# Two norms and the first block of the projection behind each: chunk by chunk through four open groups

## What is computed

```python
for i in range(DEPTH):
    mod_x = (silu_c @ w_mod[i] + b_mod[i])[:, None, :]
    mod_c = silu_cc @ w_mod[i] + b_mod[i]
    sh_x, sc_x, g_x = jnp.split(mod_x, 3, axis=-1)
    sh_c, sc_c, g_c = jnp.split(mod_c, 3, axis=-1)
    hx = rms_norm(x, norm_g[i]) * (1.0 + sc_x) + sh_x
    hc = rms_norm(ctx, norm_g[i]) * (1.0 + sc_c) + sh_c
```

## Time and profile before

| what | value |
|---|---|
| time of the kernel before, median of 3 | 1863.05 us |
| time of the profiled execution | 1862.72 us |
| its span | 1860.9 us |
| mean granted TensorE clock over the span | 0.989 of full speed |
| TensorE busy with matmuls | 1739.1 us, 93% |
| VectorE / ScalarE / GpSimd busy | 35% / 29% / 4% |
| chain that ended last | TensorE 71%, issue 12%, VectorE 6%, ScalarE 5%, DMA 4% |

### The profile page before, as it was taken

The page is one execution under the profiler, slowest core; times in us unless marked ns, Lnnn a source line. Parts: engine busy times, 40 slices in busy tenths (PEclk is TensorE's granted clock), DMA queues, the critical chain, the costliest instruction groups (busy, mean ns, idle before and its releaser), DMA issues.

```text
span 1860.9 us, 37427 instructions
## 1 busy us (share of the span) xinstructions
PE 1739.1 (93%) x16339; PEld 1117.6 (60%) x16339; DVE 649.8 (35%) x1122; ACT 530.9 (29%) x920; POOL 65.2 (4%) x64
## 2 busy tenths in 40 slices
PE   6999998999989989999988999999999999988886
PEld 3776677886668779998876454435435344423323
DVE  3664855235775765556664001010000100000001
ACT  3435834334564654334443000001000010000001
POOL 0120000011200000000001000000000000000000
PEclk9999999999999999999999999999999999999999
DMA  8362014753424635555529999999999999999996
GB/s 329 135 227 90 2 62 157 222 167 85 80 79 156 188 122 183 194 189 190 183 110 365 326 415 423 413 424 411 425 414 423 387 408 424 410 425 414 424 422 273
DMA packets 166923, 501.33 MB, mean 269 GB/s; under 512 B 27000, under 2 KB 54048, under 8 KB 150384
## 3 DMA queue, kind: packets, MB, share of 16 engines
q1 hardware_dynamic: 163824, 491.82, 70.4%
q0 software_dynamic: 1888, 6.62, 1.1%
q10 hardware_dynamic: 1056, 0.57, 0.1%
HBM read 496.84 MB, written 2.12 MB: 268 GB/s over the span
## 4 chain that ended last, share of the span: by engine, by line
PE 71%; issue 12%; DVE 6%; ACT 5%; DMA 4%; SPq 1%; POOL 1%; ACTq 0%; POOLq 0%; DVEq 0%
PE bank L2581 21%; PE bank L2021 10%; PE bank L2023 10%; PE bank L2022 10%; PE bank L2574 8%; DMA ring_t<-in_e_w 2%; ACT w_hi L844 1%; SPq L757 1%; DMA ring_h<-in_e_w 1%; DVE w_lo L1244 1%; PE bank L2200 1%; PE bank L2189 1%; PE bank L2214 1%; PE bank L2043 1%; PE bank L2527 1%
## 5 line engine op out<-in xcount | busy, mean ns | idle before, releaser
L1244 DVE TENSOR_TENSOR w_lo<-raw,w_hi 128x2048 fp32r<-128x2048 f32 x98 | 224.7, 2295 | 196.0 <-ACT w_hi L844 195.9
L2021 PE MATMUL bank<-h_hi,w_hi 128*128 128x256 f32 (+1 forms) x864 | 261.8, 303 | 4.9 <-DVE w_lo L1244 3.1
L2023 PE MATMUL bank<-h_hi,w_lo 128*128 128x256 f32 (+1 forms) x864 | 258.8, 300 | 0.0
L2022 PE MATMUL bank<-h_lo,w_hi 128*128 128x256 f32 (+1 forms) x864 | 258.6, 299 | 0.0
L844 ACT ACTIVATE w_hi<-raw 128x2048 fp32r<-128x2048 f32 x98 | 186.8, 1909 | 160.2 <-PE bank L2023 111.5
L2581 PE MATMUL bank<-ring_w,xe 128*32 128x512 f32 (+1 forms) x1920 | 188.3, 543 | 9.7 <-DMA ring_w<-in_e_w 9.6
L2021 PEld LDWEIGHTS bank<-h_hi,w_hi 128*128 128x128 f32 x864 | 165.8, 192 | 14.0 <-DVE w_lo L1244 5.7
L2022 PEld LDWEIGHTS bank<-h_lo,w_hi 128*128 128x128 f32 x864 | 165.8, 192 | 5.6 <-issue 0.2
L2023 PEld LDWEIGHTS bank<-h_hi,w_lo 128*128 128x128 f32 x864 | 165.7, 192 | 5.0
L1873 DVE TENSOR_TENSOR act_f<-act_s,bank 128x512 f32<-128x512 f32 (+1 forms) x40 | 22.7, 616 | 402.8 <-PE bank L2581 402.8
L2581 PEld LDWEIGHTS bank<-ring_w,xe 128*32 128x32 f32 x1920 | 61.6, 111 | 134.4 <-issue 106.2
(11 more groups left out here) (344 smaller groups left out, 2174.3 us busy)
## 6 DMA issues: line engine op xcount, KB each, us to landing
ring_w<-in_e_w SPq DMA_DIRECT2D x72, 1024.0 KB, 18.1
ring_h<-in_e_w SPq DMA_DIRECT2D x64, 1024.0 KB, 17.9
ring_t<-in_e_w SPq DMA_DIRECT2D x48, 1024.0 KB, 15.3
raw<-in_e_w SPq DMA_DIRECT2D x40, 1024.0 KB, 22.5
ring_w<-in_e_w SPq DMA_DIRECT2D x48, 768.0 KB, 13.8
raw<-in_w SPq DMA_DIRECT2D x33, 1024.0 KB, 5.1
raw<-in_w_qkv SPq DMA_DIRECT2D x24, 1024.0 KB, 5.1
ring_h<-in_e_w SPq DMA_DIRECT2D x32, 768.0 KB, 17.6
```

Of the source, the lines that this page charges most:

```text
L1244: nc.vector.tensor_tensor(w_lo[:, split_slot(m), :], raw_unit(m), w_hi[:, split_slot(m), :].bitcast(F32), ALU.subtract).then_inc(lo_ready, 1)
L2021: nc.tensor.matmul(out_, a_hi, b_hi, start=start, stop=False)
L2022: nc.tensor.matmul(out_, a_hi, b_lo, start=False, stop=False)
L2023: return nc.tensor.matmul(out_, a_lo, b_hi, start=False, stop=stop)
```

## The change

TensorE gets a new helper, `first_products`, which does one chunk for all four groups: in the first half the four high\*high products, then the four with the low weights, then the four with `h_lo`, with a wait ahead of each set; in the second half the three products group by group. Both norms call it between the turns. In n0 the order is: chunks 0 to 3, products 0, chunk 4, products 1, the four `w_mod` units, chunk 5, products 2, the turn, chunk 6, products 3, products 4, chunk 7, products 5 to 7. In n1: chunks 0 to 3, then products c and chunk c + 4 for c = 0 to 3, then products 4 to 7. VectorE's split in n1 moves from behind the first scaled chunk to directly behind the diagonals. The filler ahead of the buffer `ring_t` grows from 1618 to 1622 elements. The code of ScalarE, GpSimd and SyncE stays.

```diff
--- before.py
+++ after.py
@@ -443,7 +443,7 @@
         slot_token = sb("slot_token", [P, 8], U32)
         token_id = diag[:, 0, 0:TT]
         slot_row = xs[:, TT, :]
-        sb("gap_before_ring_t", [P, 1526 + 92])
+        sb("gap_before_ring_t", [P, 1622])
         ring_t = sb("ring_t", [P, 3, UW])
 
 
@@ -1345,6 +1345,8 @@
             def norm(st, tiles, scale, shift, read_before, midway=None, early=None):
                 if st != "n0":
                     norm_diag(st, tiles)
+                if st == "n1":
+                    split(beyond(last_unit["a_out"], 2))
                 if read_before is not None:
                     wait_used(dve, read_before)
                 width = tiles * P
@@ -1654,8 +1656,7 @@
             residual("a_out", "a", 4, lambda t: t // TT)
 
 
-            norm("n1", 4, lambda c, w: gain[:, 1, c, w:w + 1], lambda c, w: mod[:, 1, c, w:w + 1], last_unit["a_out"], None,
-                 lambda: split(beyond(last_unit["a_out"], 2)))
+            norm("n1", 4, lambda c, w: gain[:, 1, c, w:w + 1], lambda c, w: mod[:, 1, c, w:w + 1], last_unit["a_out"])
             for pos in range(7):
                 split(beyond(step_unit("b_in", pos, 1), 2))
                 if pos == 4:
@@ -2074,11 +2075,6 @@
                                                 start=True, stop=True)
                     last.then_inc(stage_sem["transposed"], 1)
 
-            def norm(st, tiles):
-                pe.wait_ge(*reached(st, "diag", tiles))
-                norm_chunks(st, tiles, range(CH))
-                pe.wait_ge(*reached(st, "h_lo", CH // 2))
-
             def late_norm(st):
 
                 for c in range(CH):
@@ -2134,6 +2130,45 @@
                 if half:
                     ins.then_inc(product, 1)
                 elif i == blocks_of[name][pos] - 1:
+                    ins.then_inc(w_used, 1)
+
+            def first_products(name, st, half, c):
+
+                m, k = step_unit(name, 0, half), 4 * half + c
+                hi, lo = unit_view(w_hi, m, 4), unit_view(w_lo, m, 4)
+                g0 = group_at[name]
+
+                def one(part, i):
+                    h = h_lo if part == 2 else h_hi
+                    w = lo if part == 1 else hi
+                    own = slice(i * P, (i + 1) * P)
+                    start, stop = (half, c, part) == (0, 0, 0), (half, c, part) == (1, 3, 2)
+                    if name == "a_in":
+                        return nc.tensor.matmul(bank[i][:], h[:, k, own], w[:, c, :], start=start, stop=stop)
+                    return nc.tensor.matmul(bank[i][:, 0:TOK], w[:, c, own], h[:, k, 0:TOK], start=start, stop=stop)
+
+                if half:
+                    pe.wait_ge(lo_ready, splits_before(m + 1))
+                    pe.wait_ge(*reached(st, "h_lo", k + 1))
+                    for i in range(4):
+                        for part in range(3):
+                            ins = one(part, i)
+                        if c == 3:
+                            ins.then_inc(product, 1)
+                    return
+                pe.wait_ge(hi_ready, splits_before(m + 1))
+                pe.wait_ge(*reached(st, "h_hi", k + 1))
+                for i in range(4):
+                    if c == 0 and g0:
+                        pe.wait_ge(emptied[emptied_by(g0 + i - 4)[0]], emptied_by(g0 + i - 4)[1])
+                    one(0, i)
+                pe.wait_ge(lo_ready, splits_before(m + 1))
+                for i in range(4):
+                    one(1, i)
+                pe.wait_ge(*reached(st, "h_lo", k + 1))
+                for i in range(4):
+                    ins = one(2, i)
+                if c == 3:
                     ins.then_inc(w_used, 1)
 
             def linear(name, blocks, forms, after=None, st=None, between=None, begin=0):
@@ -2345,17 +2380,22 @@
 
 
             pe.wait_ge(*reached("n0", "diag", 4))
-            norm_chunks("n0", 4, range(CH - 1))
-            for i in range(4):
-                half_group("a_in", 0, 0, i, ("rows", i), None, "n0" if i == 0 else None)
-                if i == 0:
-                    mod_units(*mods_between["a_in", 0])
-                if i == 1:
-                    turn_mod(1)
+            norm_chunks("n0", 4, range(4))
+            first_products("a_in", "n0", 0, 0)
+            norm_chunks("n0", 4, [4])
+            first_products("a_in", "n0", 0, 1)
+            pe.wait_ge(*reached("n0", "h_lo", 4))
+            mod_units(*mods_between["a_in", 0])
+            norm_chunks("n0", 4, [5])
+            first_products("a_in", "n0", 0, 2)
+            turn_mod(1)
+            norm_chunks("n0", 4, [6])
+            first_products("a_in", "n0", 0, 3)
+            first_products("a_in", "n0", 1, 0)
             pe.wait_ge(sem("mod_ready"), 2)
-            norm_chunks("n0", 4, [CH - 1])
-            for i in range(4):
-                half_group("a_in", 0, 1, i, ("rows", i), None, "n0" if i == 0 else None)
+            norm_chunks("n0", 4, [7])
+            for c in range(1, 4):
+                first_products("a_in", "n0", 1, c)
 
             def turn_a(cb):
                 mods_done("a_in", cb)
@@ -2394,15 +2434,23 @@
 
 
             pe.wait_ge(sem("gate_ready"), 4)
-            norm("n1", 4)
+            pe.wait_ge(*reached("n1", "diag", 4))
+            norm_chunks("n1", 4, range(4))
+            for c in range(4):
+                first_products("b_in", "n1", 0, c)
+                norm_chunks("n1", 4, [c + 4])
+            for c in range(4):
+                first_products("b_in", "n1", 1, c)
+
             def after_b_in(pos):
                 mods_done("b_in", pos)
                 if pos == 3:
                     pe.wait_ge(sem("mod_row_ready"), 6)
                     spread_gates(0, 4)
 
+            after_b_in(0)
             linear("b_in", 7, lambda pos: (cols(TOK), cols(TOK), cols(2 * TOK), cols(2 * TOK), cols(TOK), cols(TOK), rows(4))[pos],
-                   after_b_in, "n1")
+                   after_b_in, begin=1)
             attention_b()
```

## The result

After the change the kernel takes 1869.28 us (median of 15 runs, 1865.88 to 1871.68), before 1862.99 (15 runs, 1861.12 to 1865.78). The ratio is 1.0032, 95% interval 1.0025 to 1.0039: slower by 0.32%, 6.0 us. The profiled execution took 1869.87 us, its span is 1868.0 and its mean granted clock 0.987.

A forecast was written before the change was run, and what follows sets the result against it. It took TensorE to bound the first 400 us, with chunk 7's chain to a w_mod load deciding behind n1. Terms 0.7 + 0.1 + 1.9 + 1.3 = +4.0 us gave 1867.0; range 1862 to 1870, the forecast's own 1865.9 to 1868.

The forecast's parts named there:

- n0, the load: Behind n0's block 0: w_mod load lands later, so its unit starts at 63.5 instead of 62.8; +0.7, bounds 0 and +1.1.
- n0, the copies: Block 0's groups end together, so copies and VectorE's chain start 2.9 us later, mostly absorbed; +0.1, bounds 0 and +0.4.
- n1, the load: Behind n1: late chunk 7 delays the second w_mod load, landing at 329.5 instead of 327.6; +1.9, bounds +1.5 and +2.3.
- n1, the clock: Behind n1's new 4.7 us wait the clock falls, some 3 us at the slower pace; +1.3, bounds 0 and 2.
- What bounds the kernel: TensorE's delay in the first 400 us reaches the end whole; the chain ending last behind n1 bypasses TensorE's products.
- Chunk 7: Its turns come later: in n0 at 51.4 instead of 49.24 (+2.2), in n1 at 317.1 instead of 313.47 (+3.6).
- The moved split: VectorE's split in n1 takes 2.29 us and fits its 2.31 us idle, so the first scaled chunk starts as before.
- The fall behind n0: Rival: the clock also falls after n0's new wait of about 1.9 us; +5.5, 1868.5; chance 0.16.
- The slowing by bank cycling: Rival: cycling four PSUM banks slows products, n1's 96 to 0.21 us each; +8.6, 1871.7; chance 0.02.
- The other side: Rival: waits filled and nothing late in either norm; -0.9 and -2.2, together -3.1, 1859.9; chance 0.14.
- The chances: Whole kernel, 0.2% (3.7 us) as threshold: slower 0.48, within 0.48, faster 0.04.

The follow-up runs named there:

- e1: Kernel before with only the change's new order of n0, n1 as before: 1866.1 us, ratio 1.0007.
- e2: Kernel before with only the change's n1 (TensorE's order and VectorE's moved split), n0 as before: 1867.81 us, ratio 1.0029.
- e5: As e1, chunk 7 still turned behind chunk 4's products, but the second half's chunks 5 to 7 multiplied group by group: ratio 0.9999.
- e6: As e1, but chunk 7 turned ahead of chunk 4's products and the second half's chunks 5 to 7 multiplied group by group: ratio 0.999.
- e11: As e10, but n1 turns chunk 4, multiplies chunk 0, turns chunks 5 to 7, then multiplies chunks 1 to 3: 1858.51 us, ratio 0.9981.
- e10: Kernel before with e6's n0 and VectorE's split in n1 moved behind the diagonals, TensorE's n1 order as before: 1860.18 us, ratio 0.9982.
- e4: The change's n1 alone (as e2), but chunks 4 to 7 turned right behind chunk 0's products: 1862.94 us, ratio 1.0.
- e7: As e2, but the two w_mod units behind block 0 multiplied only after the first half of block 1: 1866.12 us, ratio 1.0018.
- e8: e6's n0; n1 turns chunk 4 ahead of chunk 0's products, chunks 5 to 7 right behind, w_mod pair placed as in e7: 1864.22 us, ratio 1.0003.
- e9: As e1, but chunk 7 turned ahead of chunk 4's products, the last products still chunk by chunk: ratio 1.0017.
- e3: Kernel before with only VectorE's split in n1 moved right behind the diagonals, TensorE's order as it was: 1861.5 us, ratio 0.9993.

## Why the prediction was right in its sign and short in its size

The forecast was +4.0 us, 1867.0; the ratio says +6.0, the median 1869.28. The wide range (1862 to 1870) holds it by 0.7 us, the forecast's own (1865.9 to 1868) does not. Term by term, each measured where its part ran alone:

| term | predicted | measured | from |
|---|---|---|---|
| n0, the load | +0.7 | +0.3 | e1: 63.03 against 62.73 |
| n0, the copies | +0.1 | +2.2 | e1: the rest of +2.48 at n1's start |
| n1, the load | +1.9 | +1.35 | e2: 25.77 against 24.42 |
| n1, the clock | +1.3 | +2.1 | e2: the rest of +3.49 |
| sum | +4.0 | +6.0 | |

Only the first term lies within its own bounds (0 to 1.1); n1's load came out under them (1.5 to 2.3), the other two above. That this sum meets the 6.0 of the ratio is in part luck: each part comes from one execution, and e1's shift, 2.4 us at n1, goes down to 0 (at 1003 us) before it is 3.4 at the end.

- **What bounds the kernel.** Right: a delay in the first 400 us reaches the end. e2 shows it best, where the shift is 3.4 us at 386 us and 3.4 at the end (3.3 to 4.2 in between); in the change it swings between 3.2 and 8.1 on the way. And n1's chain, not TensorE's products, set the next stage. The late load was named at both places, with its links; 1.73 and 4.36 us of wait stand where some 1.9 and 4.7 were forecast. All `h_lo` waits are gone.
- **Chunk 7.** 51.22 in e1, 51.4 forecast. In the profiled execution of the change it came at 49.64, since the clock did not fall at 26 us there. In n1 it moved by 3.46 us, 3.6 forecast. The moved split was covered to the hundredth: VectorE's split ends in time for the first scaled chunk, which starts at 307.83 with no wait.
- **n0, the copies: the step that failed.** "VectorE waits for TensorE once in between, which halves the shift", and so +0.1 with bounds 0 and +0.4. The start was forecast right (2.9 us later, in e1 59.11 against 56.14). The shift was not halved on the way to where it counts. That wait of VectorE exists, 1.41 us, but it stands behind ScalarE's last copy of block 1. VectorE's and ScalarE's timelines before, then ScalarE's of e1:

```profile
88.27 0.69 DVE L1627 TENSOR_TENSOR prob_t<-work,rope 128x512 f32<-128x512 f32 x1 [1.41 <-PE bank L2375]
```

```profile
86.94 0.60 ACT L1057 ACTIVATE prob<-bank 128x512 f32<-128x512 f32 x1 [3.28 <-DVE work L1615]
...
88.21 2.07 ACT L1075 ACTIVATE q_a<-bank 128x512 f32<-128x512 f32 x4
```

```profile
89.90 0.60 ACT L1057 ACTIVATE prob<-bank 128x512 f32<-128x512 f32 x1 [4.29 <-DVE work L1615]
...
90.88 2.07 ACT L1075 ACTIVATE q_a<-bank 128x512 f32<-128x512 f32 x4
```

So 2.97 us at the chain's first tile are still 2.96 at ScalarE's last copy of block 1 (89.90 in e1, 86.94 before). And I looked for slack only where VectorE's splits release loads. The slack that mattered was ScalarE's: its copy waits for VectorE, the row and `q_a` stand behind that copy in its queue, and TensorE's turn behind block 1 wants `q_a`. That place had nothing to spare (the first `q_a` copy, from 88.21, ends near 88.8, and TensorE's fourth turn began at 88.95), so the shift came through: ScalarE's `q_a` starts at 90.88 in place of 88.21, and n1's turns 2.48 us later, 0.3 of it from the load. e5 and e6 show it from the other side: with the groups ending one by one the wait is 1.09 and 0.47.
- **n1, the load.** +1.9 forecast, +1.35 measured: it was issued 1.6 us later, and landed 0.2 sooner.
- **n1, the clock.** Right in kind, short in size: 3 us at half pace were assumed; 4.8 of 6.8 us fell on work. In place of 1.3 it costs 2.1, just outside the bound of 2.
- **The rivals.** The fall behind n0 came in the profiled execution, at 90.6 us and behind the turn, not behind the load of block 0; in e1 it did not come behind a longer wait. So it costs about 1.5 us in some executions. The slowing by bank cycling did not happen: in the window from 313 to 325 us above, with four open groups, TensorE is busy 12.00 of 12 us at a clock of 1.00, and 48 products from 320.17 to the unit at 326.09 take 5.9 us, as in the earlier trace rows. The section "A second HAM failure mode: psum-queue depth-cycling" of the Trainium skill, "TensorE: Matmul & The Clock Gate", tells of TensorE idling between groups; by the window above that condition is not met here. The other side, waits filled and nothing late, needed chunk 7 early in both norms. e6 is that case in n0, 1.9 us faster by the ratio (3.5 to 0.4) where the rival said 0.9. In n1 it said 2.2, and e11 is not told from e10; in e4 the unit came 0.3 sooner, too little to keep what is filled. The chances do not quite add up: their parts give 0.49 within and 0.03 faster, where 0.48 and 0.04 are written.

## What to carry to other kernels

Filling a wait of the busiest engine is a gain only if what stands behind the filled piece does not move back: before reordering, follow the last tile (here chunk 7) through every queue behind it, ScalarE's as well as VectorE's and the loads', down to the next instruction of the busiest engine that wants it. Keep the work that starts the next stage's chain ahead of the filler, and let groups end one after the other where their consumer works on one at a time. Moving the product that frees a load's slot moved the wait here to the next load (e7, e8).

## What the runs showed of the hardware

- **The granted clock fell with only short waits of TensorE ahead of it, and not in every execution.** From 24 to 26 us on, around the first of n0's turns, it was low for 3.4 us in the profiled executions of before, e1, e7, e8, e9 and e10 (6 of 13), and not in those of the change, e2, e3, e4, e5, e6 and e11, although up to there TensorE's instructions are the same. Of the waits of TensorE from 20 us up to there the longest was 1.05 us (e10) where it fell and 0.97 (e2) where it held.
- **What such a fall costs depends on the slack behind it.** In the order of before, TensorE's turns of 26 us are ahead of VectorE. Without the fall it waits 1.28 us for `h_lo` (e3, below), with it 0.46, and chunk 7 is turned at 49.08 or 49.24. In the filled order there is no such wait, and the fall costs its full 1.5 us: chunk 7 at 51.22 (e1) or 49.64 (the change), at 48.41 (e10) or 46.97 (e6). So the gain of filling n0's waits is itself larger when the clock holds.

```profile
24.78 3.81 PE L2074 MATMUL bank<-diag,xs 128*128 128x128 f32 x32 [0.54 <-DVE diag L1312]
29.87 1.16 PE L2074 MATMUL bank<-diag,xs 128*128 128x128 f32 x8 [1.28 <-DVE h_lo L1360]
```

- **At a wait of about 2 us the fall can come or not, and the wait's length does not decide it.** It came within waits of TensorE of 2.48 (e4), 2.53 (e8), 2.59 (e7), 4.36 (the change) and 4.40 us (e2), and up to 1.3 us behind waits of 1.78, 2.13 (the change) and 3.12 (e9). It did not come at 2.25 (e1), 1.73 (the change) and 1.57 (e1). One and the same wait shows it best: n2's, 2.04 or 2.05 us for `h_lo` (at 543.02 before), has a fall within it or up to 1.3 us behind it in 11 of the 13 profiled executions, and none before and in e2; a wait of 1.93 near 246 us has one in e5 alone. What decides is open. These falls and those of the later stages go with a spread of 4 to 10 us between runs of one kernel, so a single pair of executions (here +7.15) can be a microsecond or more away from the ratio (+6.0).
